# Two unused strips in SBUF: the low weights' ring 320 bytes higher, everything above it 512 bytes

## The chip, the cores and the metric

The kernel runs as one program on 1 core of a Trainium2 chip. The metric is the device time in microseconds; the median over several runs of the same program is compared.

## The reference, cut to what matters

Two residual layers over 256 tokens of width 1024, in float32. Layer 0 mixes with sparse and dilated attention, layer 1 with stick-breaking attention; after each mixer stands a gated feed-forward block with a causal convolution of width 3. Nearly all the arithmetic is products of activations with weights:

```python
for layer in range(DEPTH):
    y = rmsnorm(h, norm_g[layer, 0])
    if layer % 2 == 0:
        y = even_mixer(y, even_w_in[i], even_w_out[i], ...)   # (256 x 1024) @ in, ... @ out
    else:
        y = odd_mixer(y, odd_w_in[i], odd_w_out[i])
    h = h + rmsnorm(y, norm_g[layer, 1])
    y = conv_ffn(rmsnorm(h, norm_g[layer, 2]), ffn_w_up[layer], ...)   # 1024 -> 5632 -> 2816 -> 1024
    h = h + rmsnorm(y, norm_g[layer, 3])
```

## The kernel before

**Weights in units.** All large weights lie in HBM as 103 units of 128 partitions x 2048 float32 (1 MB each). Each unit goes through three rings of four slots in SBUF: SP's queue loads it into `raw`; ScalarE rounds it to float32r into `whi` (L413); VectorE writes the rest of each weight, `raw - whi`, into `wlo` (L778). The first two units go in pieces (L883), two later ones in halves (L789). Both splits run `LOOK = 2` units ahead of TensorE, and SP reloads a slot of `raw` once `wlo` of the unit that lay there is written.

**Products.** Activations are held in the same way, as a rounded part and a rest (`xpair` = `xhi` and `xlo`; in the feed-forward block `hid_hi` and `hid_lo`). A product is the sum of three: high x high, low activations x high weights, high activations x low weights. Where tokens are the output's rows, these are L1380, L1382 and L1381, with 512 weight columns streamed past 128 activation columns that are held in the array (L1452 and L1507 are the same for the first chunk of a stage and the first two units). Where channels are the output's rows, the weights are held in the array and activations are streamed: L1423 streams `xhi` and `xlo` together (512 columns) past `whi`, L1430 streams `xhi` alone (256 columns) past `wlo`, 16 of each per unit.

**Stages.** in0 (18 units), out0 (3), up0 (22), down0 (11), in1 (12), out1 (4), up1 (22), down1 (11), one after another. In the up stages ScalarE and VectorE also do the convolution (L659, L665, L1160, L1171, L1178), and GpSimd multiplies gate and value (L1328) and forms `hid_lo` (L1330). In the stick-breaking attention TensorE streams `sb_sphi` and `sb_splo` past a triangle of ones (L1901, L1903). The order on every engine is written out by hand with semaphores; nothing in it depends on a tensor's place.

**Places.** Tensors are placed one after another in the order in which the code names them, at multiples of 32 bytes. Counted from the start of `h` in each partition, in bytes:

| tensor | starts at | bytes | who writes it / who reads it |
|---|---|---|---|
| `h`, `xn`, `xpair` | 0, 8192, 16384 | 8192, 8192, 16384 | |
| `raw` | 32768 | 32768 | DMA / ScalarE, VectorE |
| `whi` | 65536 | 32768 | ScalarE / VectorE, TensorE |
| `wlo` | 98304 | 32768 | VectorE / TensorE |
| `vbuf`, `qkT` (attention) | 131072, 141312 | 10240, 18432 | |
| small tables, then `t12`, `xb_parts` or `probs`, `probsT` or `sb_sp`, `sb_sphi`, `sb_splo` | 159744 up; `sb_sphi` at 173984, `xb_parts` at 179616, `probs` at 164768 | | |
| `hid_hi`, `hid_lo`, `conv`, `act_g`, `hidf` (feed-forward, over the attention's space) | 131072 up, to 192512 | 61440 | |

The constants (`c_gpre` and so on) are placed from the other end, and 640 bytes lie free between the two at the fullest point. Within the weight rings every operand begins at a multiple of 512 bytes from its ring's start (a slot is 8192 bytes, a block of 512 columns 2048, 128 columns 512).

Of the kernel before, what the change touches and what calls it, by code (L numbers as in the profile page):

```python
# [23 lines left out]
P = 128  # L24
# [56 lines left out]
def build(nc, x, weights, wgate, cmpw2, pe2, gpre, gpost, convw, rope, ropec, cmask, rows, masks, gcol, tri,  # L81
          out):
    ctx = ExitStack()
    with ctx:
# [3 lines left out]
        def sb(name, shape, dt=F32, c=ctx):  # L88
            return c.enter_context(nc.sbuf_tensor(name, shape, dt))
# [5 lines left out]
        xhi, xlo = xpair[:, :, 0, :], xpair[:, :, 1, :]  # L95
        raw = sb("raw", [P, RING, UNIT])
        whi = sb("whi", [P, RING, UNIT], F32R)
        wlo = sb("wlo", [P, RING, UNIT], F32R)

        def top(name, shape, dt=F32):  # L100
            return ctx.enter_context(nc.sbuf_tensor(name, shape, dt, side="right"))
# [1977 lines left out]
```

## Time and profile before

| | |
|---|---|
| median of 3 runs | 657.37 us (657.18 to 657.45) |
| profiled execution | span 655.8 us, 9975 instructions |
| TensorE (PE) | busy 646.6 us, 99% |
| VectorE (DVE) | busy 460.1 us, 70% |
| ScalarE (ACT) | busy 385.1 us, 59% |
| GpSimd (POOL) | busy 163.8 us, 25% |
| chain that ended last | 93% PE |

The span is taken from the first to the last instruction of one profiled execution; the times are those of other executions of the same program. Busy time of PE is the union of matmuls that overlap in the pipeline, so the length of one (389 ns for 512 columns) is longer than the distance from one to the next; the chain of work shows the distance.

### The profile page before, as it was taken

What the parts mean: (1) busy time and instruction counts of PE and PEld (TensorE: products, weight loads), DVE (VectorE), ACT (ScalarE), POOL (GpSimd) and SP (SyncE); (2) the same over time, 40 slices, a digit from 0 to 9 for tenths busy, and PEclk for the clock granted to TensorE, in tenths of its full rate; (3) what the DMA queues carried; (4) which work ended last, traced back from release to release, by engine and by line L of the source; (5) the groups of instructions that cost most, each with busy time, mean ns of one, the idle gap of its engine ahead of it and who ended that gap; (6) DMA issues with size and microseconds to landing.
All of it is one profiled execution on the core that took longest, in us unless ns stands there. A gap on an engine that the chain in (4) does not pass through costs nothing.

```text
span 655.8 us, 9975 instructions
## 1 busy us (share of the span) xinstructions
PE 646.6 (99%) x3572; PEld 539.4 (82%) x3574; DVE 460.1 (70%) x627; ACT 385.1 (59%) x561; POOL 163.8 (25%) x123
## 2 busy tenths in 40 slices
PE   9999999999999999999999999999999999999996
PEld 6888887577888888888888888777888888888885
DVE  6498766877697878786457645676688788886532
ACT  7556355865757667666335535765567676767330
POOL 0323300001053444441001000680123434343000
PEclk9999999999999999999999999999999999999999
DMA  8987633004456363637652663304255554544601
GB/s 350 339 296 284 228 129 129 1 6 189 132 198 245 133 249 131 236 149 268 242 196 69 253 240 144 129 1 192 97 184 200 182 202 168 216 151 177 248 1 64
DMA packets 18971, 115.60 MB, mean 176 GB/s; under 512 B 2911, under 2 KB 3453, under 8 KB 6013
## 3 DMA queue, kind: packets, MB, share of 16 engines
q1 hardware_dynamic: 17789, 111.52, 45.7%
q10 hardware_dynamic: 1152, 3.67, 1.7%
q8 instruction: 20, 0.33, 0.2%
q14 instruction: 10, 0.08, 0.0%
HBM read 114.14 MB, written 1.05 MB: 176 GB/s over the span
## 4 chain that ended last, share of the span: by engine, by line
PE 93%; DVE 2%; POOL 2%; ACT 1%; issue 1%; DVEq 0%; POOLq 0%
PE ps L1423 27%; PE ps L1430 14%; PE ps L1380 11%; PE ps L1381 11%; PE ps L1382 11%; PE ps L1452 5%; PE ps L1507 2%; POOL sb_splo L1352 1%; PE ps L1751 1%; PE ps L1635 1%; PE ps L1371 1%; PE ps L1901 1%; PE ps L1679 1%; PE ps L1601 1%; PE ps L1738 1%
## 5 line engine op out<-in xcount | busy, mean ns | idle before, releaser
L778 DVE TENSOR_TENSOR wlo<-raw,whi 128x2048 fp32r<-128x2048 f32 x99 | 227.0, 2325 | 72.7 <-ACT whi L413 72.6
L413 ACT CAST whi<-raw 128x2048 fp32r<-128x2048 f32 x99 | 185.7, 1916 | 48.6 <-PE ps L1382 42.0
L1423 PE MATMUL ps<-xpair,whi 128*128 128x512 f32 x768 | 183.4, 391 | 0.0
L1423 PEld LDWEIGHTS ps<-xpair,whi 128*128 128x128 f32 x768 | 141.2, 188 | 27.6
L1430 PEld LDWEIGHTS ps<-xpair,wlo 128*128 128x128 f32 x768 | 98.5, 191 | 3.7
L1430 PE MATMUL ps<-xpair,wlo 128*128 128x256 f32 x768 | 99.6, 283 | 0.0
L1328 POOL TENSOR_TENSOR hidf<-act_g,conv 128x512 f32<-128x512 f32 x22 | 76.1, 3460 | 85.0 <-ACT act_g L671 85.0
L1380 PE MATMUL ps<-whi,hid_hi 128*128 128x512 f32 x176 | 68.5, 389 | 0.0
L1381 PE MATMUL ps<-wlo,hid_hi 128*128 128x512 f32 x176 | 68.5, 389 | 0.0
L1382 PE MATMUL ps<-whi,hid_lo 128*128 128x512 f32 x176 | 68.5, 389 | 0.0
L1380 PE MATMUL ps<-whi,xpair 128*128 128x512 f32 x168 | 67.7, 403 | 0.0
L1382 PE MATMUL ps<-whi,xpair 128*128 128x512 f32 x168 | 65.7, 391 | 0.0
L1381 PE MATMUL ps<-wlo,xpair 128*128 128x512 f32 x168 | 65.6, 390 | 0.0
L1282 POOL TENSOR_TENSOR rstd<-ms,mhalf 128x1 f32<-128x1 f32 x16 | 8.8, 551 | 212.0 <-DVE ms L842 179.1
L659 ACT COPY xn<-ps 128x512 f32<-128x512 f32 x40 | 21.5, 590 | 61.5 <-PE ps L1430 61.5
L1171 DVE SCALAR_TENSOR_TENSOR conv<-ps,c_conv,conv 128x255 f32<-128x255 f32 x88 | 38.2, 478 | 17.0 <-ACT conv L665 16.8
L665 ACT ACTIVATE conv<-ps,c_conv 128x256 f32<-128x256 f32 x88 | 42.6, 566 | 9.8 <-DVE ps L1160 9.8
L1330 POOL TENSOR_TENSOR hid_lo<-hidf,hid_hi 128x512 f32 (+1 forms) x22 | 28.7, 1304 | 74.7 <-ACT hid_hi L675 74.7
L1160 DVE TENSOR_TENSOR ps<-ps,xn 128x512 f32<-128x512 f32 x40 | 25.9, 694 | 24.6 <-ACT xn L659 24.6
L1382 PEld LDWEIGHTS ps<-whi,hid_lo 128*128 128x128 f32 x176 | 33.0, 188 | 6.9
L1380 PEld LDWEIGHTS ps<-whi,hid_hi 128*128 128x128 f32 x176 | 33.0, 188 | 6.8
L1381 PEld LDWEIGHTS ps<-wlo,hid_hi 128*128 128x128 f32 x176 | 33.1, 188 | 6.7
(197 smaller groups left out, 788.2 us busy)
## 6 DMA issues: line engine op xcount, KB each, us to landing
raw<-in_weights SPq DMA_DIRECT2D x101, 1024.0 KB, 5.0
c_gpost<-in_gpost ACTq DMA_DIRECT2D x4, 512.0 KB, 5.0
raw<-in_weights SPq DMA_DIRECT2D x3, 512.0 KB, 6.8
c_gpre<-in_gpre ACTq DMA_DIRECT2D x3, 512.0 KB, 4.3
h<-in_x SPq DMA_DIRECT2D x2, 512.0 KB, 3.8
out<-h SPq DMA_DIRECT2D x4, 256.0 KB, 2.0
raw<-in_weights SPq DMA_DIRECT2D x2, 256.0 KB, 4.8
t<-in_masks SPq DMA_DIRECT2D x1, 512.0 KB, 12.1
```

What stands on the lines that cost most here:

```text
L413: act.copy(whi[:, slot, :], raw[:, slot, :]).then_inc(hi_done, 1)
L665: act.activation(conv[:, par, m, :], ps[:, b0 + m, 0:SEQ], ACT.Identity, scale=c_conv[:, bass.ds(cofs + (4 * m + 2), 1)], bias=c_conv[:, b ...
L778: dve.tensor_tensor(wlo[:, slot, :], raw[:, slot, :], whi[:, slot, :].bitcast(F32), ALU.subtract).then_inc(lo_done, 1)
L1171: ins = dve.scalar_tensor_tensor(conv[:, par, m, 1:SEQ], ps[:, b0 + m, 0:SEQ - 1], c_conv[:, bass.ds(cofs + (4 * m + 1), 1)], conv[:, par, ...
L1328: pool.tensor_tensor(hidf[:, par], act_g[:, par], conv[:, par, 2:4, :], ALU.mult).then_inc(up_hf, 1)
L1330: pool.tensor_tensor(hid_lo[:, tile, :], hidf[:, par], hid_hi[:, tile, :].bitcast(F32), ALU.subtract).then_inc(up_lo, 1)
L1380: pe.matmul(out, s_hi, m_hi, start=start, stop=False, skip_group_check=shared)
L1381: pe.matmul(out, s_hi, m_lo, start=False, stop=False, skip_group_check=shared)
L1382: return pe.matmul(out, s_lo, m_hi, start=False, stop=stop, skip_group_check=shared)
L1423: pe.matmul(ps[:, b0 + m, :], whi[:, slot, cols], xpair[:, kt].rearrange("p a c -> p (a c)"), start=kt == 0, stop=kt == KT - 1, skip_group ...
L1430: ins = pe.matmul(ps[:, b0 + m, 0:SEQ], wlo[:, slot, cols], xhi[:, kt, :], start=False, stop=kt == KT - 1, skip_group_check=True)
L1452: ins = pe.matmul(ps[:, bank + t, :], x[:, kt, t * P:(t + 1) * P], w[:, u % RING, b * BLK:(b + 1) * BLK], start=kt == 0 and x is xhi and w ...
```

## The change

Two tensors are allocated that nothing reads or writes: `low_gap`, 80 float32 (320 bytes) a partition, ahead of `wlo`, and `stage_gap`, 48 float32 (192 bytes), behind it. `wlo` then starts at 98624, and `vbuf`, `hid_hi` and all above them at 512 more than before. `h`, `xn`, `xpair`, `raw`, `whi` and the constants keep their places. No instruction, wait, size or order is touched.

```diff
         raw = sb("raw", [P, RING, UNIT])
         whi = sb("whi", [P, RING, UNIT], F32R)
+        sb("low_gap", [P, 80])
         wlo = sb("wlo", [P, RING, UNIT], F32R)
+        sb("stage_gap", [P, 48])
```

## Rows read from the trace of the kernel before

**Rows 1.** The page: the span's 40 slices, and the chain that ended last.

```profile
PE   9999999999999999999999999999999999999996
DVE  6498766877697878786457645676688788886532
PEclk9999999999999999999999999999999999999999
PE 93%; DVE 2%; POOL 2%; ACT 1%; issue 1%; DVEq 0%; POOLq 0%
```

**Rows 2.** What TensorE waited for: releaser, us in total, times, longest.

```profile
PE ps L1500 <- POOL c_mask L1264: 1.3, 1, 1.3
PE ps L1901 <- POOL sb_splo L1352: 1.1, 2, 0.6
```

**Rows 3.** The chain in up0: start us, us, line and count.

```profile
264.32 3.65 PE ps L1423 x16
267.97 1.91 PE ps L1430 x16
269.89 3.65 PE ps L1423 x16
...
281.02 1.16 PE ps L1423 x5
```

**Rows 4.** The chain in down0, one matmul of 512 columns a row.

```profile
333.99 0.23 PE ps L1382
334.21 0.23 PE ps L1380
334.44 0.23 PE ps L1381
...
338.29 0.23 PE ps L1380
```

**Rows 5.** Instructions that read or write `wlo`: ns minimum/median/maximum, first and last start.

```profile
L1430 PE MATMUL ps<-xpair,wlo x768: 277/283/283, 178.7 to 590.1; 128*128 128x256 f32 x192
L1381 PE MATMUL ps<-wlo,hid_hi x176: 389/389/397, 286.7 to 649.6; 128*128 128x512 f32 x176
L1381 PE MATMUL ps<-wlo,xpair x168: 387/389/402, 21.2 to 463.8; 128*128 128x512 f32 x168
L778 DVE TENSOR_TENSOR wlo<-raw,whi x99: 2269/2286/3384, 15.8 to 630.5; 128x2048 fp32r<-128x2048 f32 x99
L1452 PE MATMUL ps<-wlo,xpair x48: 387/389/398, 162.7 to 475.5; 128*128 128x512 f32 x48
L1751 PE MATMUL ps<-wlo,xb_parts x32: 278/278/288, 39.1 to 64.5; 128*64 128x256 f32 x32
L1507 PE MATMUL ps<-wlo,xpair x16: 389/391/503, 8.5 to 18.9; 128*128 128x512 f32 x16
L883 DVE TENSOR_TENSOR wlo<-raw,whi x5: 680/1217/1220, 7.7 to 14.2; 128x1024 fp32r<-128x1024 f32 x3, 128x512 fp32r<-128x512 f32 x2
L789 DVE TENSOR_TENSOR wlo<-raw,whi x4: 1225/1226/1227, 142.8 to 150.8; 128x1024 fp32r<-128x1024 f32 x4
```

**Rows 6.** The tile `hid_lo`: TensorE's reads and GpSimd's writes, same columns.

```profile
L1382 PE MATMUL ps<-whi,hid_lo x176: 388/389/389, 286.9 to 649.8; 128*128 128x512 f32 x176
L1330 POOL TENSOR_TENSOR hid_lo<-hidf,hid_hi x22: 1298/1305/1311, 190.6 to 600.5; 128x512 f32 x20, 128x512 fp32r<-128x512 f32 x2
```

**Rows 7.** The chain in the stick-breaking attention: 384 and 128 columns of `sb_sphi`, `sb_splo`.

```profile
442.17 0.18 PE ps L1901
442.34 0.06 PE ps L1903
```

**Rows 8.** Transposes, 128 columns streamed from `probs` and from `xn`.

```profile
L1635 PE MATMUL ps<-c_identf,probs x80: 270/273/329, 103.1 to 142.8; 128*128 128x128 f32 x80
L1371 PE MATMUL ps<-c_identf,xn x48: 270/273/329, 160.5 to 471.9; 128*128 128x128 f32 x48
```

**Rows 9.** Busy time by stretch: PE, PEld, DVE, ACT, POOL, clock, DMA share, GB/s.

```profile
30.00:100.00 70.00, 69.94 (x378) 58.97 (x378) 58.50 (x76) 37.12 (x30) 17.79 (x10) 1.00 0.65 240
198.00:300.00 102.00, 102.00 (x570) 89.44 (x570) 80.28 (x108) 70.72 (x92) 42.95 (x20) 1.00 0.50 189
```

**Rows 10.** The tile `hidf`: GpSimd's product beside VectorE's splits.

```profile
L1328 POOL TENSOR_TENSOR hidf<-act_g,conv x22: 2602/3402/4817, 182.6 to 597.2; 128x512 f32<-128x512 f32 x22
```

## The prediction

> **What bounds the kernel.** I read the slices and the chain first. TensorE is busy in every slice but the last, at the full granted clock (2.4 GHz), and 93% of the chain that ended last is TensorE's [rows 1]. Then TensorE's own waits: the two largest are 1.3 us at the start and 1.1 us in the attention [rows 2]. So of 655.8 us nearly all is matmuls one behind the other, and the question is what sets the distance from one matmul to the next. VectorE, ScalarE, GpSimd and the DMA queues matter only if one of them grows so much that TensorE has to wait.
>
> The distance comes from the chain, not from the length of one matmul, since they overlap. In up0 a unit is 16 matmuls of 512 columns and 16 of 256. Three of L1423's runs start at 264.32, 269.89 and, with the row of 281.02, three periods later: (281.02 - 264.32) / 3 = 5.57 us a unit [rows 3]. The columns alone, 16 x 512 + 16 x 256 = 12288 at 2.4 GHz, take 5.12 us. The rest, 0.45 us over 32 matmuls, is 14 ns each. In down0 19 steps take 338.29 - 333.99 = 4.30 us, so 226.3 ns each (the starts are rounded to 10 ns), 13 ns over the 213.3 ns of 512 columns [rows 4]. What a place in SBUF could change is this 13 to 14 ns, or add to it.
>
> **The change, part by part.** It adds and removes no instruction, no wait and no DMA, so nothing moves in any queue (SP's, ACT's and POOL's included) and nothing new is queued behind anything. Three things differ: where `wlo` begins (320 bytes past a multiple of 512 as counted from `h`, where it was on a multiple), where all above it begins (512 bytes higher, so at the same remainder by 512, 256, 64 and 32 as before), and how far the two lie from `raw` and `whi`. Before, `raw`, `whi` and `wlo` lie exactly 32768 bytes apart, so the three streams of a split on VectorE have the same remainder by 32768, and so do ScalarE's two. ScalarE's pair stays as it is.
>
> *TensorE reading wlo.* 768 + 176 + 168 + 48 + 32 + 16 = 1208 matmuls [rows 5]. Is there something in their time that comes from the place? Three comparisons say no. First, low against high: L1381 with `wlo` and L1382 with `whi` are both 389 ns in the median [rows 5, 6] and both take one step of the chain of the same length [rows 4]; 16 runs of L1430 take 1.91 us, 119.4 ns each, 106.7 for the columns and 13 over [rows 3]. Second, other neighbours: in up0 the ring's slots are written by VectorE and ScalarE in some of the matmuls and not in others, yet the minimum and the median of L1430 differ by 6 ns only, the maximum by none [rows 5]. Third, other remainders: `sb_sphi` lies at 173984, which is 416 past a multiple of 512 and 32 past one of 64. Its 384 columns take 0.18 us and its 128 columns 0.06 us [rows 7], together 0.24 us for 512 columns in two matmuls: 213 ns for the columns and 13 or 14 ns over for each of the two, as on the grid. Transposes of `probs` (164768, again 32 past a multiple of 64) and of `xn` (a multiple of 512) have the same 270/273/329 ns [rows 8]. I take 0 ns a matmul. Both ends: the widest gap between medians of one shape at different places is 2 ns (391 of L1507 against 389) [rows 5]; a gap of that size on all 1208 is 1208 x 2 ns = 2.4 us, as a loss or as a gain.
>
> [...]
>
> *Places 512 higher.* `hid_hi` is held in the array or streamed past, `vbuf`, `qkT`, `conv`, `probs` and others move with it. Their remainders stay, and the reads of `hid_lo` are the most regular in the trace, 388/389/389 [rows 6]. 0 us; the same 2 ns on the 352 reads of `hid_hi` in L1380 and L1381 and the 176 of `hid_lo` would be 528 x 2 ns = 1.1 us either way. Three loads land above the gap (`t12`, `c_wg`, `c_rows`), once, at the start; they come out at the same remainders. 0 us.
>
> *VectorE writing wlo.* A split of 2048 elements takes 2286 ns in the median, one of 1024 1226 ns, one of 512 680 ns at the least [rows 5]. From 512 to 1024 that is 546 ns, from 1024 to 2048 1060: about 1.04 to 1.07 ns an element at every size. [...] So 0 to gain. If it did change, it is hidden: in up0 VectorE has 102 - 80.28 = 21.7 us idle, over 102 / 5.57 = 18.3 units, 1.19 us a split; in in0 70 - 58.50 = 11.5 us over the about 15 units that 70 us hold, 0.77 us a split [rows 9]. A split would have to take a third longer before TensorE waits; a gain there gives nothing at all. With the cover gone, each further 0.1 us a split over the 40 units of in0, up0 would be 4 us.
>
> *The rest.* ScalarE's operands stay where they are. GpSimd's product L1328 takes 3402 ns where L1330, of the same size, takes 1305 [rows 6, 10]: it stands behind a VectorE split that is under way.
>
> [...]
>
> **The sum.** 0 on TensorE, 0 elsewhere: the profiled span stays 655.8 us, and the median, which stands 1.6 us above the span, 657.4 us. The measurement tells about 0.2% from no change, that is 1.3 us; a place effect would need 1.3 us / 1208 = 1.1 ns in each matmul that reads `wlo` to be seen.
>
> **The rivals.**
>
> *Low weights off the common grid read slower.* A remainder of 320 could make the array's loads or the streamed reads of `wlo` dearer than `whi`'s: a run of 2048 bytes then touches five stretches of 512 bytes instead of four. For it: no row has a 512-column stream at such a remainder. Against it: rows 7 and 8. Price by the widest gap, 2 ns: +2.4 us, 659.8 us. It decides from 1.1 ns a matmul. Chance 5%, with a small part for VectorE's splits growing beyond their cover, which the profile gives no reason for.
>
> *Common remainders cost something now.* If a part of the 13 ns is a clash between the stream being read, the weights being loaded and the two writers, because all lie on the same remainder by 32768, moving `wlo` away takes it off. For it: all that the weight products read and write lies on that grid, so they show no other case. Against it: the surcharge is the same in down0 as in up0, though other tensors are held and streamed, and the same for `sb_sphi`, which is off the grid [rows 3, 4, 7]; matmuls beside writers and without are alike. The ceiling is 1208 x 13 ns = 15.7 us, but I price it at the same 2 ns: -2.4 us, 655.0 us. Chance 5%.
>
> *It shows on VectorE alone.* Splits become shorter or longer by tens of ns and TensorE does not notice: 657.4 us, the same as the forecast, told apart only in the trace. I count it with no change, together 90%.
>
> **How the numbers follow.** No change within 0.2%: 90%. Faster 5%, slower 5%. The range: the likeliest case alone, with the spread of runs (0.27 us from the lowest to the highest) and half a part in a thousand for another execution, is 656.9 to 657.9. The two tails together are 10%, so the range need not reach 655.0 or 659.8; I take about 1 us to either side, 656.4 to 658.4, which also holds place effects of up to 0.8 ns a matmul.
>
> **What would show it.** Right: L1430 and L1381 still at 283 and 389 ns, a unit of up0 still 5.57 us, L778 still near 2286 ns, TensorE's waits still under 3 us, the same chain. Wrong: a period in up0 of 5.55 or 5.59 us, or L1381's steps in down0 parting from L1380's; then the grid matters and my reading of rows 7 and 8, which have few columns, was too weak. A wait of TensorE on L778 would mean that VectorE's cover was smaller than the stretch's sum says.

## The result, and the profile after

The changed kernel takes 660.99 us (660.91 to 661.07, 4 runs) against 657.41 us (657.18 to 657.55, 4 runs) on the same chip: ratio 1.0054, 95% interval 1.004 to 1.0068. It is 3.6 us slower, where the prediction had 657.4 us, a range of 656.4 to 658.4 and 5% for slower. The profiled execution has a span of 659.1 us. All line numbers of the code below the two strips are 2 higher.

First what did not move. The page's section 2, then what TensorE waited for, both of the kernel after:

```profile
PE   9999999999999999999999999999999999999996
PEclk9999999999999999999999999999999999999999
```

```profile
PE ps L1502 <- POOL c_mask L1266: 1.3, 1, 1.3
PE ps L1903 <- POOL sb_splo L1354: 0.9, 2, 0.6
PE ps L1619 <- ACT probs L539: 0.4, 1, 0.4
```

TensorE is still busy in every slice but the last, at the full clock (granted clock 1.000), and its waits are those of [rows 2] within 0.2 us. So the 3.6 us are in the matmuls themselves. The tile `wlo` and, last line, the tile `hid_lo` (ns minimum/median/maximum, first and last start):

```profile
L1432 PE MATMUL ps<-xpair,wlo x768: 279/281/283, 180.0 to 592.0; 128*128 128x256 f32 x192
L1383 PE MATMUL ps<-wlo,hid_hi x176: 388/395/398, 287.3 to 652.9; 128*128 128x512 f32 x176
L1383 PE MATMUL ps<-wlo,xpair x168: 387/395/398, 21.3 to 466.1; 128*128 128x512 f32 x168
L780 DVE TENSOR_TENSOR wlo<-raw,whi x99: 2269/2287/3395, 15.9 to 633.3; 128x2048 fp32r<-128x2048 f32 x99
L1454 PE MATMUL ps<-wlo,xpair x48: 388/394/398, 163.9 to 477.9; 128*128 128x512 f32 x48
...
L1384 PE MATMUL ps<-whi,hid_lo x176: 390/393/402, 287.6 to 653.1; 128*128 128x512 f32 x176
```

Against [rows 5] the medians of the 512-column matmuls went from 389 to 393 to 395 ns, and that also where `whi` is streamed, which did not move (last line, against [rows 6]). The 256-column ones went from 283 to 281: faster. VectorE's split is as before, 2287 against 2286 ns. The chain of the kernel after, in up0 and in down0 (start us, us, line):

```profile
265.11 3.65 PE ps L1425 x16
268.76 1.89 PE ps L1432 x16
270.65 3.65 PE ps L1425 x16
...
281.73 1.39 PE ps L1425 x6
```

```profile
333.90 0.24 PE ps L1382
334.14 0.23 PE ps L1383
334.37 0.23 PE ps L1384
...
338.31 0.23 PE ps L1383
```

In up0 three units now take 281.73 - 265.11 = 16.62 us, 5.54 each, against 5.57 in [rows 3]. In down0 19 steps take 338.31 - 333.90 = 4.41 us, 232.1 ns each, against 226.3 in [rows 4]. That is the story in small: in down0, where weights are streamed, a matmul costs over 5 ns more, and in up0, where low weights are held, one of 256 columns costs about 1.6 ns less.

The sum over the traces goes by the distance from one matmul's start to the next (distances of 260 ns and more, 47 before and 44 after, left out; means in ns):

| matmuls | count | before | after | us |
|---|---|---|---|---|
| streamed `whi`/`wlo` past `hid_hi`, `hid_lo` | 527 | 226.8 | 232.0 | +2.8 |
| streamed `whi`/`wlo` past `xpair` | 696 | 228.7 | 231.6 | +2.0 |
| `xhi` past held `wlo`, 256 columns | 768 | 119.6 | 118.0 | -1.2 |
| `xhi` and `xlo` past held `whi` | 768 | 228.4 | 228.3 | -0.1 |

Together +3.5 us, against 3.6 measured.

Within the steady state the shape changed as well. Before, down0 is a train of 226, 227, 227 ns. After, the distances run through 224, 226, 229, 233, 232, 231, 236, 231, 229, 233, 235, 233, 231, 236, 241 and over again: no single wait, but a pattern that never settles. They do so with VectorE and ScalarE busy or idle alike: where the hidden rows are held, the mean is 232.0 ns with VectorE at work throughout and 232.0 ns with VectorE idle, 231.8 and 232.1 ns for ScalarE.

### The profile page after: what moved, and what is told of

Same layout as the page of the kernel before. It is cut to its first block, busy times and chain, and to the rows that moved or that the text cites. A ratio compares the mean times of both kernels' runs of the same rounds, so it can differ in the third digit from the quotient of the medians.

```text
span 659.1 us, 9977 instructions
## 1 busy us (share of the span) xinstructions
PE 650.3 (99%) x3574; PEld 538.4 (82%) x3574; DVE 460.2 (70%) x627; ACT 384.9 (58%) x561; POOL 161.5 (24%) x123
## 4 chain that ended last, share of the span: by engine, by line
PE 93%; DVE 2%; POOL 2%; ACT 2%; issue 1%; POOLq 0%; DVEq 0%; ACTq 0%
PE ps L1425 27%; PE ps L1432 14%; PE ps L1382 12%; PE ps L1384 11%; PE ps L1383 11%; PE ps L1454 5%; PE ps L1509 2%; POOL sb_splo L1354 1%; PE ps L1753 1%; PE ps L1637 1%; PE ps L1373 1%; PE ps L1681 1%; PE ps L1903 1%; PE ps L1603 1%; PE ps L1740 1%
## 5 line engine op out<-in xcount | busy, mean ns | idle before, releaser
L780 DVE TENSOR_TENSOR wlo<-raw,whi 128x2048 fp32r<-128x2048 f32 x99 | 227.0, 2323 | 75.6 <-ACT whi L415 75.4
L1382 PE MATMUL ps<-whi,hid_hi 128*128 128x512 f32 x176 | 69.3, 394 | 0.0
L1382 PE MATMUL ps<-whi,xpair 128*128 128x512 f32 x168 | 68.2, 406 | 0.0
L1382 PEld LDWEIGHTS ps<-whi,hid_hi 128*128 128x128 f32 x176 | 33.1, 188 | 7.7
```

The source lines that it names most:

```text
L780: dve.tensor_tensor(wlo[:, slot, :], raw[:, slot, :], whi[:, slot, :].bitcast(F32), ALU.subtract).then_inc(lo_done, 1)
L1382: pe.matmul(out, s_hi, m_hi, start=start, stop=False, skip_group_check=shared)
```

## The experiments

The theories at the start: A, the low weights' own place, off the 512-byte grid of the ring they alternate with in the stream; B, the hidden rows and all else that is 512 bytes higher; C, a clash of TensorE's reads with the writes of ScalarE and VectorE, whose streams lay exactly 32768 bytes apart. Bytes are counted as in the table of places, and a remainder is one by 256 unless another is named. On the grid means at a multiple of 512 bytes, where every operand of the weight products lay before. The comments in the diffs below are mine and not in the kernels.

**e1_stage512 and e2_low512: 512 bytes alone.**

```diff
+        sb("stage_gap", [P, 128])      # e1: behind wlo
```

```diff
+        sb("low_gap", [P, 128])        # e2: ahead of wlo, nothing behind it
```

> Only what lies above the low weights is 512 bytes higher, the ring of low weights stays. Theory A (it is the ring's own place, off the 512-byte grid of the ring it alternates with in the stream): 657.4 us, the 512-column matmuls of down0 226.6 ns apart. Theory B (the hidden rows and all above them, 512 bytes higher, do it): 661.0 us, 232 ns apart in down0.

> The low weights and all above 512 bytes higher, no second strip. Theory A, by the remainder modulo 512 or less: 657.4 us. If the remainder counts by a larger power of two (1024 to 32768, the whole distance to the ring of high weights): away from 657.4, some 661 us. Theory B: 661.0 us.

657.45 us (ratio 0.9999, 0.9989 to 1.0008) and 657.46 us (0.9999, 0.9989 to 1.0009), with 226.5 to 227.0 ns in down0. Theory B is out, and so is a rule by the exact distance of 32768 between the rings.

**e3_low320: the first strip alone.**

```diff
+        sb("low_gap", [P, 80])         # wlo and all above it 320 higher
```

> The first strip alone: low weights and all above them 320 bytes higher. Theory A: 661 us, as with both strips, with 118 ns a matmul of 256 columns in up0 and 232 ns in down0 and in0; what lies above (hidden rows held in the array) may add or take some tenths. Theory B, by the 512: cannot say; 657.4 if only a place of 512 higher hurts.

661.77 us (1.0066, 1.0049 to 1.0083); 118.0 ns for the 256 columns. As A has it, though down0 is dearer than the 232 ns that it named, and the three kinds part: 235.4, 237.9 and 230.0 ns. The dearest, L1382 with `wlo` past `hid_hi`, is the one in which the two now share a remainder:

```profile
L1382 PE MATMUL ps<-wlo,hid_hi x176: 397/399/400, 286.9 to 653.7; 128*128 128x512 f32 x176
```

**e4_pair320: both rings of weights.**

```diff
+        sb("pair_gap", [P, 80])        # ahead of whi
...
+        sb("stage_gap", [P, 48])       # behind wlo
```

> Both weight rings, high and low, 320 bytes higher, all above 512. Theory A in the form that the two rings have to share a remainder: 657.4 us, 226.6 ns. Theory A in the form that the streamed weights and the held activations have to share a remainder: slower than the change, over 661 us, since now every streamed operand differs from the activations, and 118 ns or less for the 256-column matmuls. Theory C (writers on ScalarE and VectorE clash with TensorE's reads): now ScalarE's two operands differ too, so the lengths of its splits would move from 1915 ns.

658.56 us (1.0015, 1.0006 to 1.0025). The chain in up0:

```profile
264.32 3.73 PE ps L1425 x16
268.05 1.82 PE ps L1432 x16
```

16 matmuls on `whi` take 3.73 instead of 3.65 us, 16 on `wlo` 1.82 instead of 1.91 [rows 3]: 233.1 and 113.9 ns. Neither form of A that I had written down fits: if it were enough that the two rings share a remainder, the time would be 657.4, and "over 661" was wrong. What is left to try is the remainder between the held and the streamed operand of each matmul, with different signs for different shapes. ScalarE's splits stayed at 1910 ns in the median against 1915, so C has nothing to show here.

**m1_grid: TensorE alone, 64 pairs of places.** No weights, no splits, no other engine at work while a group runs; one profiled execution. One of 128 such groups:

```python
for i in range(32):
    ins = pe.matmul(ps[:, i % 8, 0:512], hold64[:, i % 4, :], flow192[:, i % 2, 0:512], start=True, stop=True)
```

> TensorE alone: no weights loaded, no splits, nothing of the reference computed; the input is copied to the output. 64 groups of 32 matmuls of 512 columns and 64 of 256, all float32r: the held 128 columns start at a remainder of 0, 64, ... 448 by 512, the streamed ones likewise, and a pause stands between groups. Theory A1 (the load of the held columns and the stream of the others share SBUF, and their difference in remainder sets the distance between matmuls): the distances depend on the difference alone, 227 ns (120 for 256 columns) at no difference and up to some 235 (or 114 to 118) elsewhere. Theory A2 (what counts is the jump from one streamed block to the next, whi to wlo and back): within a group the remainder never jumps, so all 64 are 227 ns. Theory C (writers' clash): no writer here, all 227 ns.

Mean distance in ns over the last 23 of each group; rows are the remainder by 512 of the held block, columns that of the streamed one:

```
512 columns    0     64    128    192    256    320    384    448
    0      226.7  228.9  232.3  233.2  226.7  228.9  232.3  233.2
   64      233.4  227.1  228.9  232.3  233.2  226.7  228.9  232.3
  128      232.7  233.4  227.1  229.0  233.5  233.4  227.1  229.0
  192      229.0  232.3  233.4  227.1  229.0  232.3  233.4  227.1
256 columns
    0      120.0  117.8  118.6  113.3  120.0  117.8  118.6  113.3
   64      113.3  120.0  117.8  118.9  113.3  120.0  117.8  118.9
  128      120.0  117.8  120.0  113.3  118.6  113.3  120.0  113.3
  192      117.8  118.6  113.3  120.0  113.3  118.6  113.3  120.0
```

The rows for held blocks at 256 to 448 repeat these four within 0.2 ns. The chain of this kernel, for a held block at 0 and streams at 64, 128, 192 and 256 (lines 95, 97, 99, 101), start and length of 32 matmuls after a pause:

```profile
33.15 7.62 PE ps L95 x32
...
41.04 7.72 PE ps L97 x32
...
49.02 7.75 PE ps L99 x32
...
57.04 7.56 PE ps L101 x32
```

The table is one of diagonals: for 512 columns the distance hangs on the streamed place less the held place, by 256 (226.7 to 227.1 ns at no difference, 228.9 to 229.0 at 64, 232.3 to 233.5 at 128, 233.2 to 233.4 at 192), and 64 bytes are enough to see it. A2 and C, which had 227 ns everywhere, are out as the only cause: with one engine running and no jump between streams there is an effect. It is not the whole one: a difference of 64 gives 228.9 ns here, where the changed kernel has 232.0 in down0. On 256 columns the order is another one: no difference is the dearest, 192 the cheapest by 6.7 ns. There the diagonals have exceptions in the rows of 128 and 192: a difference of 64 gives 113.3 ns in three places where others have 117.8, and at 128 a difference of 192 gives 117.8 once and one of 128 gives 120.0 once. Whether the places or the groups ahead make these exceptions m1_grid cannot tell.

**e5_low64, e6_low128, e7_low256, e8_low192: the ring of low weights alone, in the whole kernel.** Each has a `low_gap` of so many bytes and a `stage_gap` that fills up to 512, as

```diff
+        sb("low_gap", [P, 16])         # e5; 32 in e6, 64 in e7, 48 in e8
...
+        sb("stage_gap", [P, 112])      # e5; 96, 64, 80
```

> Low weights 64 bytes higher, all above 512. Theory A (remainder by 512 counts): off the grid already, between 657.5 and 662 us. If only multiples of 128 or 256 off do harm: 657.4.

> Low weights 128 bytes higher, all above 512. If the remainder by 128 is what counts (320 is 64 past a multiple of 128): 657.4 us. If the remainder by 512: away from 657.4, either side.

> Low weights 256 bytes higher, all above 512. If the remainder by 256 or less counts: 657.4 us. If by 512: away from it, either side.

> Low weights 192 bytes higher, all above 512. Theory A (remainder by 256): 120 to 118 ns for L1430's 256 columns (the class of 64 when low weights are held), down0 between 229 and 233 ns a matmul: 658.5 to 661.5 us, and not 657.4. Theory that only odd multiples of 64, or only 64 and 128 past the grid, do harm: 657.4.

| `wlo` higher by | us | ratio, 95% interval | `whi`, `wlo` past `hid_hi`, `whi` past `hid_lo`, ns | 256 columns, ns |
|---|---|---|---|---|
| 64 | 660.61 | 1.0048, 1.0032 to 1.0065 | 231.4, 232.3, 232.4 | 118.0 |
| 128 | 661.53 | 1.0061, 1.0044 to 1.0077 | 230.8, 229.6, 233.0 | 120.4 |
| 192 | 659.84 | 1.0038, 1.0023 to 1.0052 | 229.5, 229.3, 228.5 | 117.9 |
| 256 | 657.53 | 1.0001, 0.9992 to 1.0011 | 226.8, 227.1, 226.4 | 119.6 |
| 320 (the change) | 660.99 | 1.0054, 1.004 to 1.0068 | 231.4, 232.1, 232.5 | 118.0 |

By 256: 320 behaves as 64, and 256 as nothing. 128 and 192 are both off 657.4, so it is not the remainder by 128 that counts, and not 64 and 128 alone.

**m2_patterns: the kernel's own sequences, TensorE alone.** The core, with the places varied:

```python
(hold0[:, i % 4, :], flow0[:, i % 2, :]), (hold0[:, i % 4, :], flow64[:, i % 2, :]), (hold0[:, (i + 1) % 4, :], flow0[:, i % 2, :])
```

> TensorE alone again, nothing of the reference computed. First 16 groups of 512 and 16 of 256 columns with the held block at remainder 0 and the stream 0, 16, ... 240 bytes on: Theory A1 with classes of 64 bytes expects the same distance for 0 to 48, for 64 to 112 and so on (227, 229, 232, 233 ns); a finer rule would give other values between. Then down0's pattern, 16 times (hold, high), (hold, low), (next hold, high), low 0, 64, 128, 192 bytes on: A1 as a sum of classes expects means of 227, 227.4, 228.5, 228.9 ns; the full kernel had 232 in all three with 64, so if jumps between streams count too, 232 here at 64. Then up0's pattern, 16 matmuls of 512 and 16 of 256 in turn, without a pause, for high weights at 0 to 192 and low weights at 0 to 192: at 0 and 0 228 and 120, at 0 and 64 228 and 118, at 64 and 64 233 and 114, as in the full kernels.

The chain of this kernel: down0's sequence with low weights at 0 and at 64 (lines 134, 136), then up0's with them at 0 (142 to 147), and at 64 (149 to 154):

```profile
214.97 11.19 PE ps L134 x48
226.43 11.41 PE ps L136 x48
...
267.16 3.65 PE ps L144 x16
270.81 1.91 PE ps L145 x16
...
284.42 3.65 PE ps L151 x16
288.07 1.89 PE ps L152 x16
```

Means: 227.2 and 231.9 ns in down0's sequence (231.0 at 128, 229.3 at 192), and in up0's 228.4 with 119.6 on the grid, 228.3 with 117.9 at 64, 233.1 with 113.6 when high and low weights both stand at 64. The full kernels had 226.8 and 232.0; 228.4, 119.6; 228.3, 118.0; 233.1, 113.9. (All these are means of the distances under 260 ns.) TensorE alone gives these kernels' numbers to within half a nanosecond, and with them the pattern of 15 distances: behind L136 they run through 224, 226, 229, 232, 233, 231, 235, 231, 229, 234, 235, 232, 231, 237, 241. The plain sum of classes, 227.4 at 64, was wrong: one odd stream in three slows all three. So of the 5.2 ns that down0 lost, the pair's difference by itself explains 0.7 (227.4 less 226.7); the rest comes only where streams of different remainders alternate. What e3_low320 has in down0, 237.9 ns at no difference and 234.4 in the mean, lies above every value of m1_grid, and no group has its sequence. The same pair also has different values after different neighbours (held 64, streamed 0, 256 columns: 113.6 ns where the 512-column matmuls between have high weights at 64 too, 117.9 where these are on the grid). With high weights at 128 and low ones at 64 the same 16 matmuls even change from one round to the next (lines 206, 208, 210):

```profile
421.14 1.89 PE ps L206 x16
...
426.75 1.82 PE ps L208 x16
...
432.28 1.90 PE ps L210 x16
```

In steps of 16 bytes the stream at 0, 16, 32, 48, 64 past the held block has 226.7, 231.4, 233.3, 233.2 and 229.2 ns for 512 columns. So 64 bytes are no natural step, only the one I had tried; that half of the expectation fails.

**e9_all320: everything from the left, 320 bytes.**

```diff
+        sb("first_gap", [P, 80])       # ahead of h
```

> Every tensor placed from the left, activations, both weight rings, hidden rows, is 320 bytes higher; differences among them stay, only the constants from the other end stay. Theory A1 (differences of remainders count): 657.4 us, 227 and 120 ns. Theory A3 (the place itself counts, 64-byte steps against the 256-byte grid of SBUF): some 661 us, as with the change.

657.49 us (1.0002, 0.9992 to 1.0012), 226.5 to 227.0 ns in down0 and 119.6 for the 256 columns. It is differences between tensors that count, not places.

**e12_high_hid: both rings and the hidden rows.**

```diff
+        sb("pair_gap", [P, 80])        # ahead of whi, nothing behind wlo
```

> Both weight rings and all above them, the hidden rows too, 320 bytes higher; no second strip. Pairwise differences then are 0 in down0 (226.7 ns for all three, where e4_pair320 had 225.9 to 231.7), as in e4_pair320 in up0 (233.1 and 113.9) and where xpair is held (229.4 to 230.1). Against e4_pair320 that is 528 x (228.9 - 226.7) = 1.2 us less: 657.4 us. If places and not differences counted: 658.6 or more.

657.34 us (0.9995, 0.9986 to 1.0004). down0 is back at 226.7, 226.4 and 227.0 ns, up0 stays at 233.0 and 113.9, and streams past `xpair` at 229.9 and 229.3 for 228.9 and 228.2. The tile `hid_hi` of this kernel:

```profile
L1382 PE MATMUL ps<-wlo,hid_hi x176: 389/389/395, 287.0 to 649.6; 128*128 128x512 f32 x176
```

`raw` stayed where it was while both rings moved, and down0 is as before: the differences to `raw` do not count. A loss where `xpair` is held and a gain in up0 cancel: the same time as before, by another route.

**e10_up64 and e11_pads: the gain without the loss.** Slots of the low ring get 256 bytes more, and only units of L1430 are written and read 64 bytes higher in their slot. Room comes from laying `c_w2` over `pcT`, and VectorE's last round of each up stage is written out, since the units of down0 that it splits stay on the grid.

```diff
-        wlo = sb("wlo", [P, RING, UNIT], F32R)
+        wlo = sb("wlo", [P, RING, UNIT + 64], F32R)
...
-                dve.tensor_tensor(wlo[:, slot, :], raw[:, slot, :], whi[:, slot, :].bitcast(F32),
+                dve.tensor_tensor(wlo[:, slot, o:o + UNIT], raw[:, slot, :], whi[:, slot, :].bitcast(F32),
...
-                    cols = slice(b * BLK + m * P, b * BLK + (m + 1) * P)
+                    cols = slice(LOW_AT + b * BLK + m * P, LOW_AT + b * BLK + (m + 1) * P)
```

`LOW_AT` is 16 elements in e10_up64 and 0 in e11_pads.

> Every slot of the low weights' ring is 256 bytes longer, and the low weights of the channel units alone (768 matmuls of L1430) are written and read 64 bytes higher in it; all other units stay on the grid. By the groups of TensorE alone (16 matmuls of 512 columns and 16 of 256 in turn: 228.4 and 119.6 ns on the grid, 228.3 and 117.9 with the low weights at 64) it gains (119.6 - 117.9 + 0.1) x 768 = 1.4 us: 656.1 us. Rival: the remainder acts through the writers or the neighbours as well, and VectorE's shifted splits cost what TensorE gains: 657.5.

> The same kernel with a shift of 0: longer slots, one small table in another place, VectorE's last round written out, nothing off the grid. Both theories: 657.5 us. What it differs from the kernel before is the part of e10_up64's that is not the shift.

e10_up64 takes 656.14 us, ratio 0.9978 (0.9969 to 0.9987); e11_pads 657.48 us, 0.9998 (0.9989 to 1.0007). Their difference is 1.34 us, against 1.4 worked out beforehand from m2_patterns; the two kernels' own distances, 119.6 and 118.0 ns, make 768 x 1.6 ns = 1.2 us. The chain of e10_up64 in up0, and its tile `wlo`:

```profile
269.25 3.65 PE ps L1436 x16
272.90 1.89 PE ps L1443 x16
```

```profile
L1443 PE MATMUL ps<-xpair,wlo x768: 279/281/283, 178.6 to 588.5; 128*128 128x256 f32 x192
L1394 PE MATMUL ps<-wlo,hid_hi x176: 389/389/398, 285.9 to 648.1; 128*128 128x512 f32 x176
```

It has the 281 ns of the change for held low weights and the 389 ns of before for streamed ones, and is the fastest of all kernels here.

## Why the prediction was wrong

*The bound and the place to look* were right. TensorE's distances set the time, nothing else moved, and the kernel after differs in them alone. The 106.7 ns for 256 columns stand in m1_grid too: with both blocks at 0, 512 columns take 226.7 ns and 256 take 120.0, which is 106.7 ns for 256 more, 0.417 ns a column or 2.4 GHz.

*"I take 0 ns a matmul"* is the step that failed. Measured are +5.2 ns where weights stream past the hidden rows, +2.9 past `xpair`, -1.6 where low weights are held; together 3.5 us where the sum has 0. Three comparisons stood behind the 0, and each fell short in its own way. The first, low against high, compared two operands of the same remainder, so it could not see a remainder's effect, and the effect isn't tied to one operand anyway. The second looked for other engines as the partner in a clash, where m1_grid and m2_patterns have the effect with TensorE alone; minimum and median being close said only that the state was steady. The third did have operands off the grid, but read them from rows in hundredths of a microsecond: 0.18 + 0.06 us for two matmuls [rows 7] leaves several ns open in each, as much as the effect. It was also one pair picked from several. The next rows of the same chain are:

```profile
442.40 0.22 PE ps L1901
442.63 0.06 PE ps L1903
442.69 0.23 PE ps L1901
```

So here 384 and 128 columns take 0.28 to 0.29 us, some 70 ns over their columns, and "13 or 14 ns over for each" holds for the first pair of the four alone. Whether that has to do with the place no run tells; it is so in the kernel after as well. And what was counted was the stream's place from `h`, while m1_grid says that the place of the held triangle counts as much. The transposes of [rows 8] hold `probs` and `xn` and stream the identity `c_identf`: the trace names the streamed tile first, and the kernel passes it last. From start to start both take 109 ns in the median though their held blocks differ by 160 in the remainder, so nothing is seen there at 128 columns. That shape m1_grid and m2_patterns do not cover, and shapes differ even in the sign.

*The bound of 2 ns* came from rows that all lie on the grid, so it bounded nothing about leaving it. From the same rows a fair end would have been the resolution of what I had read off the grid: an estimate of some 5 ns on 1208 matmuls, 6 us. The signs of being wrong were half right: up0's period did move, to 5.54 us, but L1381's steps did not part from L1380's, since all three kinds rose together.

*The first rival* (low weights off the grid are slower) is what happened, for 5%, but not by its mechanism of more 512-byte stretches: that would have slowed only reads of `wlo`, while `whi`'s slowed alike, and held ones became faster. *The second rival*, a gain, is in the result too, 1.2 us of it, in the 256-column group, where the common grid does cost something; but its writers have no part in it, since m2_patterns has the gain without them (119.6 to 117.9 ns).

*VectorE, ScalarE, GpSimd and the DMAs* at 0 were right: 2287 ns a split against 2286, and waits of TensorE below 3 us. That a split has nothing to gain was an estimate, and no run shows what a clash of its streams would cost; what the runs show is a median of 2284 to 2287 ns in every full kernel, wherever `wlo` lies. Nor does any run show why GpSimd's product stands behind VectorE's split. The traces show that it does, before and after alike: all 22 end 1.14 to 1.16 us after the end of the split beside them (in up0 one of before runs from 261.45 to 264.85 us, the split of 261.41 to 263.69), and the median is 3402 and 3396 ns. *512 bytes higher costs nothing* was right (e1_stage512, e2_low512).

In m1_grid nothing else runs, and the distance between matmuls still moves between 226.7 and 233.5 ns for 512 columns with the places of just two operands, the held and the streamed one. Nor is a small step free: m2_patterns has 226.7 ns at 0 and 231.4 at 16 bytes.

What stays open is what happens inside. The runs show that the differences modulo 256 of held and streamed places set the distance, with steps down to 16 bytes; that it is a clash of two reads in SBUF was only argued. Why alternating remainders cost more than each difference alone, why 256 columns like another difference than 512, and why the same 16 matmuls take 1.89 us in one round and 1.82 in the next (m2_patterns, lines 206 and 208), was not settled. All of it is for float32r with 128 held columns.

## What to carry to other kernels

In a kernel whose matmuls stand back to back, the places of the held and the streamed operand belong to the schedule: keep the difference a multiple of 256 bytes for 512-column float32r streams (226.7 to 227.1 ns, against 228.9 to 233.5 at the other differences of m1_grid), and for all streams of a sequence, since one odd stream in three slows its neighbours too (227.2 to 231.9 ns in m2_patterns), and measure before adding a small tensor ahead of a big one, since a strip of 64 bytes cost 0.5% here. For other shapes try the differences in a small kernel of matmuls alone, in the order in which the full kernel issues them: that gave the full kernel's distances to half a nanosecond, while groups with one pair of places gave 228.9 ns where the kernel had 232.0. And an effect of 2% a matmul cannot be ruled out from rows rounded to 10 ns, nor from one pair of rows where the next pair reads otherwise, nor from rows that all share the property in question.

## What the runs showed of the hardware

- The distance between float32r matmuls depends on streamed place less held place modulo 256 bytes: 226.7 to 233.5 ns for 512 columns, 113.3 to 120.0 ns for 256 (m1_grid, one pair of places a group), with no other engine at work. The 512 columns follow the difference to within 0.4 ns at 0, 64 and 192 and to within 1.2 ns at 128; the 256 columns have exceptions.
- A common shift of 320 bytes changes nothing (657.49 us), nor does 256 or 512 bytes for one ring (657.53 and 657.46 us).
- The sequence counts: the same 16 matmuls of 256 columns take 113.6 or 117.9 ns each by the matmuls around them (m2_patterns), and one odd stream in three lifts all three from 227.2 to 231.9 ns.
